# Identity transposes ahead of the last row tile's turns at three norms, and six waits and pieces of work moved, in a two-block transformer kernel

## The reference

```python
def first_block(x, ...):
    h = rms_norm(x, g_mix_norm)                    # norm "mix"
    z = h @ w_in
    q_m, k_m, v_m, o_m, gates, c_q, c_kv, k_pe = split(z)
    y_a = mlstm_group(...)    # 4 heads, both directions; sigmoid(o_m) * rms_norm(h)
    y_b = mla_group(...)      # 4 heads of softmax attention on latent q, k, v
    x = x + concat([y_a, y_b]) @ w_out
    h = rms_norm(x, g_ffn_norm)                    # norm "ffn"
    return x + square(relu(h @ w_ff1)) @ w_ff2

def second_block(x, ...):
    proj = rmsnorm(x, norm_mix_g) @ w_in           # norm "mix2"
    ry = retention(...)       # 4 heads
    dy = diff_attention(...)  # 4 heads, difference of two softmaxes
    x = x + concat([ret_out, diff_out]) @ w_out
    x = x + peer(rmsnorm(x, norm_ffn_g), ...)      # norm "peer"; 16384 experts
    return rmsnorm(x, final_norm_g)
```

## Time and profile before

| | us |
|---|---|
| runs before: median of 3 | 2349.71 |
| lowest, highest | 2343.17, 2353.16 |
| profiled execution | 2352.68 |
| its span, first to last instruction | 2350.9 |
| mean granted TensorE clock over the span | 0.992 |
| PE busy | 2288.5 |
| DVE busy | 1347.7 |
| POOL busy | 1178.3 |
| ACT busy | 915.8 |

### The profile page before, as it was taken

The page is one execution under the profiler, slowest core; times in us unless marked ns, Lnnn a source line. Parts: engine busy times, 40 slices in busy tenths (PEclk is TensorE's granted clock), DMA queues, the critical chain, the costliest instruction groups (busy, mean ns, idle before and its releaser), DMA issues.

```text
span 2350.9 us, 29628 instructions
## 1 busy us (share of the span) xinstructions
PE 2288.5 (97%) x11229; PEld 1143.2 (49%) x11429; DVE 1347.7 (57%) x2765; ACT 915.8 (39%) x1095; POOL 1178.3 (50%) x558
## 2 busy tenths in 40 slices
PE   8999999999999999999999999999999999999998
PEld 4556444444444564544566444444444444444443
DVE  3668474554425545898896555555555544555555
ACT  3233342333333443111687333344444334444432
POOL 1002346655543347410000676666666666888873
PEclk9999999999999999999999999999999999999999
DMA  6031358989752239834588886666666666776641
GB/s 220 0 108 37 142 168 247 259 238 262 226 156 72 72 126 261 223 117 157 206 323 311 286 244 201 197 197 192 192 194 189 193 170 176 200 203 172 173 113 45
DMA packets 404136, 427.16 MB, mean 182 GB/s; under 512 B 276258, under 2 KB 343078, under 8 KB 392500
## 3 DMA queue, kind: packets, MB, share of 16 engines
q1 hardware_dynamic: 397684, 414.05, 58.3%
q10 hardware_dynamic: 6336, 11.54, 1.3%
HBM read 286.06 MB, written 72.37 MB: 152 GB/s over the span
## 4 chain that ended last, share of the span: by engine, by line
PE 56%; DMA 2%; POOL 1%; ACT 1%; issue 1%; DVE 1%; SPq 1%; POOLq 0%; ACTq 0%; DVEq 0%
PE ps L1860 27%; PE ps L2168 23%; PE ps L2207 3%; DMA gate_matrix<-split 1%; PE ps L2184 1%; PE ps L2185 1%; DMA ring<-in_peer_v 1%; SPq L691 1%; PE ps L2133 1%; ACT split L1382 1%; POOL u_split L955 0%; POOL split L836 0%; PE ps L2073 0%; DMA arena<-u_split 0%; POOL u_split L841 0%
## 5 line engine op out<-in xcount | busy, mean ns | idle before, releaser
L1860 PE MATMUL ps<-split,arena 128*128 128x512 bf16 x3712 | 819.7, 380 | 5.8 <-DVE consts L2940 1.6
L1860 PEld LDWEIGHTS ps<-split,arena 128*128 128x128 bf16 x3792 | 371.1, 98 | 449.5 <-issue 4.3
L2168 PE MATMUL ps<-arena 128*128 128x512 bf16 x1886 | 415.7, 379 | 2.1 <-DMA arena<-u_split 0.3
L961 POOL TENSOR_TENSOR split<-ring,split 128x1024 bf16<-128x1024 f32 x140 | 299.3, 2146 | 76.4 <-ACT split L1417 76.4
L836 POOL TENSOR_TENSOR split<-ring,split 128x4096 bf16<-128x4096 f32 x26 | 207.2, 7971 | 197.1 <-ACT split L1189 194.7
L1860 PE MATMUL ps<-arena,split 128*128 128x512 bf16 x1316 | 296.8, 381 | 5.0 <-DVE arena L2640 2.0
L2168 PEld LDWEIGHTS ps<-arena 128*128 128x128 bf16 x1920 | 187.7, 98 | 227.2 <-DMA arena<-u_split 0.8
L955 POOL TENSOR_TENSOR u_split<-ring,u_split 128x1024 bf16<-128x1024 f32 x80 | 167.7, 2127 | 191.1 <-ACT u_split L1404 191.1
L947 POOL TENSOR_TENSOR split<-ring,split 128x1024 bf16<-128x1024 f32 x44 | 92.7, 2138 | 258.1 <-ACT split L1414 258.1
L1860 PEld LDWEIGHTS ps<-arena,split 128*128 128x128 bf16 x1344 | 142.9, 107 | 150.0 <-DVE arena L2640 6.1
L1417 ACT ACTIVATE split<-ring 128x1024 bf16<-128x1024 f32 x140 | 146.3, 1054 | 172.2 <-POOL ring L971 66.6
(11 more groups left out here) (357 smaller groups left out, 3125.1 us busy)
## 6 DMA issues: line engine op xcount, KB each, us to landing
ring<-in_peer_v SPq DMA_DIRECT2D x32, 2048.0 KB, 8.3
ring<-in_peer_u SPq DMA_DIRECT2D x20, 2048.0 KB, 12.0
ring<-in_w_ff SPq DMA_DIRECT2D x16, 2048.0 KB, 8.2
gate_matrix<-split SPq DMA_DIRECT2D x16, 2048.0 KB, 7.5
arena<-gate_matrix SPq DMA_DIRECT2D x32, 1024.0 KB, 6.8
arena<-in_peer_u SPq DMA_DIRECT2D x48, 512.0 KB, 4.8
turned_table<-u_split SPq DMA_DIRECT2D x48, 512.0 KB, 5.6
ring<-turned_table SPq DMA_DIRECT2D x12, 2048.0 KB, 9.1
```

The lines of the kernel that those rows point to most:

```text
L961: pool.tensor_tensor(part_place(i, 1), block, part_place(i, 0), ALU.subtract).then_inc(v_lo, 1)
L1860: mm = pe.matmul(dst, a(k), b(k), start=n == 0, stop=n == len(terms) - 1)
L2168: mm = pe.matmul(up_bank(j), a, b, start=n == 0, stop=n == len(terms) - 1)
```

## The change

The change touches seven places. `hold(6, bank, t)` transposes the identity onto the place that the last row tile's first turn will fill, six times, right ahead of the wait for the last row tile at the norms ffn, mix2 and peer. The sigmoid of `o1` is taken in two parts: three row tiles after the fifteenth projection, the last one after the sixteenth. `out_high(0)` is cut into four pieces of 1024 columns, behind head 1, inside and behind head 2, and inside head 3. POOL's inverse roots move ahead of a split: `mlstm_rms(2)` ahead of the first low half, the one of row tile 1 (and 2) of mix2 ahead of `split_low(18)` (and of the two `pre_low` behind it), and the one of row tile 0 of peer ahead of `split_low(27)`. ACT squares row tile 1 of mix2 ahead of one conversion of a peer row. In the feed-forward the square stays in the PSUM bank, and `ff_up` waits for `ff_lo` where it waited for `ff_relu`. DVE does `mixed_probs(15)` ahead of the copies for two earlier tiles.

```diff
@@ pool, first block and mix2 @@
             mlstm_rms(1)
+            mlstm_rms(2)
             pool.wait_ge(w_hi, 1)
...
             first_low.then_inc(w_lo, 1)
-            mlstm_rms(2)
             mlstm_rms(3)
...
                 if s == 18:
                     inverse_rms(1, D, 33, 0)
+                    inverse_rms(1, D, 34, 1)
                 split_low(s, s % 4)
                 if s == 18:
-                    inverse_rms(1, D, 34, 1)
+                    inverse_rms(1, D, 35, 2)
                 for b in range(2):
                     pre_low(2 * (s - 3) + b, b)
-                    if s == 18 and b == 0:
-                        inverse_rms(1, D, 35, 2)
@@ pool, peer @@
             pre_late(SOON)
+            inverse_rms(1, D, 69, 0)
             split_low(27, 3)
-            inverse_rms(1, D, 69, 0)
@@ scalar @@
+                if t == 3:
+                    act.wait_ge(mm_out, 15)
+                    act.activation(o1[:, 0:3, :], o1[:, 0:3, :], ACT.Sigmoid).then_inc(o_sig, 1)
                 nope_rows(t)
             z_out(15)
             act.wait_ge(mm_out, 16)
-            act.activation(o1, o1, ACT.Sigmoid).then_inc(o_sig, 1)
+            act.activation(o1[:, 3, :], o1[:, 3, :], ACT.Sigmoid).then_inc(o_sig, 1)
...
                 attend_exp(4 * h + 1)
+                if h >= 2:
+                    out_high(0, slice(1024 * (2 * h - 3), 1024 * (2 * h - 2)), h == H - 1)
...
-                if h == 2:
-                    out_high(0)
+                if 1 <= h < H - 1:
+                    out_high(0, slice(2048 * (h - 1), 2048 * (h - 1) + 1024), False)
...
             split_high(18, 2, 5)
+            mix2_squares(1)
             pre_high(15, 0)
-            mix2_squares(1)
@@ tensor @@
+            def hold(n, dst_bank, t):
+                for _ in range(n):
+                    pe.transpose(bank(dst_bank)[:, t * P:(t + 1) * P], ident, ident)
...
             def row_turns(stage, src_k, rows_done, t):
+                if t == NT - 1:
+                    hold(6, turn_bank(stage, 0), t)
                 pe.wait_ge(xn_done, rows_done + t + 1)
...
                 for j in range(4):
-                    pe.wait_ge(ff_relu, 4 * g + max(j - 1, 0))
+                    pe.wait_ge(ff_lo, 4 * g + max(j - 1, 0))
@@ vector @@
-                    dve.wait_ge(o_sig, 1)
+                    dve.wait_ge(o_sig, 2)
...
-                    dve.tensor_tensor(hid[:, j % 2, :], relu[:, j % 2, :], relu[:, j % 2, :], ALU.mult).then_inc(ff_sq, 1)
+                    dve.scalar_tensor_tensor(bank(2 + j % 2), bank(2 + j % 2), 0.0, relu[:, j % 2, :], ALU.max, ALU.mult).then_inc(ff_sq, 1)
...
-                    dve.tensor_tensor(hid_lo[:, par, j, :], hid[:, j % 2, :], hid_hi[:, par, j, :], ALU.subtract).then_inc(ff_lo, 1)
+                    dve.tensor_tensor(hid_lo[:, par, j, :], bank(2 + j % 2), hid_hi[:, par, j, :], ALU.subtract).then_inc(ff_lo, 1)
...
             for i in range(H * NT + 3):
+                if i == H * NT:
+                    mixed_probs(i - 1)
...
                 if i == H * NT:
-                    mixed_probs(i - 1)
                     decayed_scores(0)
```

More of the change, by code:

```diff
@@ L242, in build @@
         relu = part(arena, 8192, 2, T)
-        hid = part(arena, 9216, 2, T)
         hid_hi = part(arena, 10240, 2, 4, T, dt=BF16)
@@ L1131, in attend_exp, with out_high @@
                                accum_out=row_sum[:, i:i + 1]).then_inc(att_exp, 1)
-            def out_high(c):
+            def out_high(c, part=slice(0, 4096), last=True):
                 act.wait_ge(ring_in[1 + c], arrived(1 + c, 1))
-                act.activation(split[:, c, 0, :], ring[:, 1 + c, :], ACT.Copy).then_inc(w_hi, 1)
+                step = act.activation(split[:, c, 0, part], ring[:, 1 + c, part], ACT.Copy)
+                if last:
+                    step.then_inc(w_hi, 1)
             for h in range(H):
```

## The result

| | before | after |
|---|---|---|
| median of 18 runs, us | 2348.47 | 2355.27 |
| lowest, highest | 2342.62, 2353.16 | 2351.64, 2358.93 |
| profiled execution, its span | 2352.68, 2350.9 | 2357.67, 2355.9 |
| mean granted clock over the span | 0.992 | 0.995 |

The ratio after to before is 1.0031, 95% interval 1.0025 to 1.0038: slower by 6.8 us of median, where 2345.4 was forecast with a range up to 2350.5. The difference is small, 0.3%, but the interval is clear of 1, and the time lies outside the range and on the wrong side.

The account below looks back on a forecast made before the run. PE, busy 97% of the span, was taken as the bound, so only its idle or lower-clock places could give time. The terms summed to -4.25, rounded to -4.3: 2345.4 us at the median, range 2337.5 to 2350.5.

Parts of the forecast that it names:

- the square in PSUM: Feed-forward: relus come on time, the first group waits, later groups wait for nothing; net +0.2, plus +1.4 for the clock.
- Rival (c): Feed-forward: POOL also stops the subtraction with one PSUM operand, 2.7 us in seven groups, +19; total 2364; chance 0.04.
- The first group: Feed-forward, between the first two ff_up: waiting for the whole chain makes a gap of 0.79 + 1.4 = 2.2 us.
- the +1.4: Feed-forward, behind the first 2.2 us gap: the clock falls and matmuls run slowly; +1.4 us, ends 0 and +2.7.
- Sigmoid: Head 0: most of the sigmoid fits ACT's idle time, PE's gap shrinks to about 0.4; -4.6 us, between -1.9 and -5.0.
- Rival (b): Head 0: the clock falls there although the gap is 0.4 us; 2.7 less gain, 2348 to 2351; chance 0.19.
- Head 3: End of head 3: POOL's low halves meet DVE's head end; -0.3 left, +0.9 for 1.2 GHz; ends -3.5 and +2.3.
- Mix2: Mix2 norm: root of row tile 1 moves ahead of split_low(18), the scaling is stopped until the split ends; -0.4 us.
- Peer: Peer norm: root of row tile 0 goes ahead of split_low(27), the scaling again falls under the split; -0.3 us.
- `mixed_probs(15)`: PE's last turn, waiting 1.75 us: the probabilities fit DVE's idle time ahead of the copies; -1.0, ends 0 and -1.75.
- Transposes: Six identity transposes at ffn, mix2 and peer shorten gaps; -0.15 at ffn, 0 at mix2 and peer, ends 0 and -2.7.
- rival (a): Whole kernel: the clock stays up and the heads keep their gain; -9.8, up to -12.5, 2337.2 to 2340; chance 0.27.

Follow-up runs that it names:

- e4_act_order: Changed kernel with ACT's high half of a group's first feed-forward tile between the two peer-row conversions, not behind both; 2339.87 us, ratio 0.9967.
- e3_ff_alone: Kernel before with only the feed-forward edits (square in PSUM, wait for ff_lo); 2362.34 us, ratio 1.0063.
- e13_all: Changed kernel plus ACT's order of e4_act_order, w_out conversion pieces one place earlier, and low half 18 ahead of mix2's squares and roots; 2334.77 us, ratio 0.9946.
- e1_sigmoid: Kernel before with only the sigmoid in two parts; 2343.83 us, ratio 0.9999.
- e7_early_pieces: e2 with the four pieces of the w_out conversion one place earlier each; 2336.25 us, ratio 0.9952.
- e10: Kernel before with only PE's wait moved from ff_relu to ff_lo, square left in SBUF; 2395.31 us, ratio 1.0203.
- e2: Changed kernel with its feed-forward edits undone; 2339.12 us, ratio 0.9965.
- e6: e2 with the first w_out conversion whole again behind head 2 and POOL's mlstm_rms(2) behind the low halves again; 2340.97 us, ratio 0.9987.
- e5_no_hold: e2 without the six identity transposes (hold) at the norms; 2341.69 us, ratio 0.9973.

## Why the prediction was wrong

**The step that failed** is the last sentence on the square in PSUM: "Inside a group the chain (relu 0.69, square 0.69, subtraction 0.69) is far below a tile's 5.2 us, so later groups wait for nothing." The chain that `ff_lo` stands for has a fourth link, ACT's high half (`ff_hi`), for which DVE waits ahead of the subtraction. For the first tile of a group that link stands in ACT's queue behind the split of the weights (3.62) and two conversions of peer rows, the second of which waits for a DMA. It took 5.5 us from the relu's end to the start of the high half, the whole chain 7.6 from 371.2, against the 5.2 that PE leaves. I listed what ACT issues for the heads, and for the feed-forward took the durations of DVE's three operations as the chain, without looking who releases each. The trace of before showed it:

```profile
332.94 0.69 DVE L2640 TENSOR_SCALAR arena<-ps 128x512 f32<-128x512 f32 x1 [4.01 <-PE ps L1860]
333.67 6.61 DVE L2642 TENSOR_TENSOR arena<-arena 128x512 f32<-128x512 f32 x1
...
336.55 0.61 ACT L1210 ACTIVATE arena<-arena 128x512 bf16<-128x512 f32 x1
```

The high half of the first tile started 2.9 us behind the relu's end there too. Only nobody waited for it: the square, held beside POOL's split, came later still, at 340.28, and PE waited for neither.

What it cost, in terms: 14.9 - 2.0 = 12.9 us of waits, and two blocks at 1.2 GHz behind gaps of 2.09 and 2.23, 12.24 instead of 10.55, 3.4 together. That is 16.3 of the 16.5 in the stretch. The prediction had 1.6 there.

**Rival (c)** had the right place, a cost near it (+19 for the groups, where the stretch grew by 16.5; its total of 2364 is 9 us too high) and "a chain longer than the 5.2 us of one tile" as its point of decision, but the wrong mechanism: line 2658 takes 0.690 to 0.691 in all 32 executions, POOL never stops it, and e4_act_order removes the waits with POOL's split where it was. At 4% it did not carry the range. The place deserved its chance from the chain's length alone.

**The first group** was right in size: a gap of 2.2 us was forecast and is 2.24, in the changed kernel and in e4_act_order. In the changed kernel the clock did not fall there (10.55 for the block behind), so the +1.4 was zero, and it fell at two other gaps of the same length. In e3_ff_alone, e4_act_order and e13_all the gap is 2.24 to 2.25 too and the clock falls (22.58 to 22.60 for 96 products instead of 20.88, 1.7 us): the +1.4 was a fair price, and that it was not paid in this execution was chance.

**Sigmoid**: -4.6 forecast, -4.93 measured, and at e1_sigmoid again. Gap 0.32 against "about 0.4". Rival (b) is out.

**Head 3**: +0.6 forecast (-0.3 and +0.9). Between the two profiles it is +2.6; over the profiled executions of five kernels of each kind the means are 86.5 and 85.5, +0.9. The mechanism came as described: the score that stood at 236.12 came 3.1 us earlier behind head 0's gain, POOL's low halves met DVE's head end, and the gap was 3.30, not 4.4, with all behind it slow. The term for the clock was drawn too small: from the turn at 237.79 to `w_out` it is 13.0 us, against 9.9 at full clock in e7_early_pieces, so 3.1 and not 0.9. In five executions of the same code it lies between 0.9 and 3.4, 2.2 on the mean, and two of them are above the end of +2.3. That the mean of the whole, +0.9, is so near the +0.6 is luck: the -0.3 beside it was drawn too small by about as much (0.9 - 2.2 = -1.3, an estimate from these means).

**Mix2**: -0.4 forecast, -0.56 between the profiles; the scaling took 5.02 us under POOL's split and ended 0.55 behind it, as said. But the nearness of the two numbers is chance: with the order of before the turns take 17.74 to 19.33 (before, e1, e3, e10), with that of the change and the transposes 15.92 to 17.57 (after, e2, e4, e6, e7), 1.7 less on the mean, and much of the spread is whether the clock fell behind the gap. **Peer**: the scaling took 5.28 under the split, as said, but PE did not wait for it. A gap of 2.51 stood only in the one profile of before; in e1_sigmoid, with the same order there, it is 0.25. The rest of the program takes 1695.6 to 1695.8 in e1, e3 and e10, which have no edit there, and 1700.8 in the profile of before. So of the -6.6 in "the rest" about 5 is that one execution and not the change, and no term from peer can be read out of these runs. **`mixed_probs(15)`**: PE's wait went from 1.75 (1.7 to 1.8 in e1, e3, e10) to 0.7 in every kernel that has the edit: -1.06, -1.0 forecast. **Transposes**: -0.15 at ffn and 0 at the other norms forecast; no effect on the time could be told.

**The sum.** With 16.3 in place of the 1.6 the forecast of -4.3 becomes +10.4, against +6.8 in the medians. What remains is not traced; it may lie in the parts that differ from execution to execution (launch, peer, the clock). Without the feed-forward the change is a gain of 9 us, near the -9.8 of rival (a), though not for its reason: the clock did fall at head 3.

## What to carry to other kernels

When a wait is moved to a later semaphore, follow the chain behind that semaphore through every engine, and read what each link's queue holds ahead of it, DMA waits too; the lateness of a link for which nobody waits is in the trace of before, in the row that names what released it. Work that must not meet a DVE operation with its operands in SBUF belongs where both engines that prepare it are idle, and as early as its data allow: cutting it in pieces only moved the wait here, to what stands behind the pieces. A gap of 2 to 3 us cost its length here and, sometimes, about as much again in slow matmuls behind it (1.7 us behind gaps of 2.1 to 2.3, up to 3.4 behind 3.30); price both, and the second with its whole spread.

## What the runs showed of the hardware that I had not expected

- A DVE operation of 128x8 elements takes 0.17 us alone and 1.98 under a POOL subtraction of 2.1 us per instruction. The prediction had no row for small operations. By the Trainium skill, page "SBUF — State Buffer", section "SBUF: two separate sides", the lock is held for the whole instruction. This row agrees, for an operation this small. The squares and subtractions with one operand in PSUM kept their 0.69 to 0.70 us beside POOL in all 32 executions each of the changed kernel, e3_ff_alone and e4_act_order.
- The same code behind the same gap does not get the same clock. After 3.13 to 3.14 us of idling at mix2 the clock stayed up in e2 and e7 (turn 0.71, the twelve products behind it 2.75); in e4 and e6 it fell behind the turn (0.71, then 4.44), in the changed kernel within it (0.92), and in e5_no_hold the whole turn was slow (1.12). After 3.30 us at head 3 the sixteen turns of `y1` took 2.02, 2.02, 2.49, 3.60 and 3.63 in five executions of identical code. Of the eight gaps of 0.57 to 2.49 us in the feed-forward of the changed kernel, the clock fell behind two, of 2.09 and 2.23; behind the first, 2.24, it stayed up, and behind the same first gap it fell in e3, e4 and e13.
- A POOL low half in four pieces takes 8.83 us where the whole takes 7.95.
